# Four gate tiles between the heads of the linear attention, and another order of the expert groups

## The reference, cut to what matters

```
h = rmsnorm(x, norm1_w) * (1 + sc1) + sh1
u, gate_b, gate_c, q, k, v, g_out, lr_f, lr_b, gate_br_conv, gate_br_gla = split(h @ w_in)
y_conv = gate_b * conv3_rows(gate_c * u)
y_gla  = gla_mixer(q, k, v, g_out, ...)          # 4 heads, 2 directions, chunks of 64
merged = sigmoid(gate_br_conv) * (y_conv @ w_br_conv) + sigmoid(gate_br_gla) * (y_gla @ w_br_gla)
x = x + g1 * (merged @ w_out)
h2 = rmsnorm(x, norm2_w) * (1 + sc2) + sh2
x = x + g2 * (sum over 8 of 64 experts: w * (silu(h2 @ w_gate_e) * (h2 @ w_up_e)) @ w_down_e  + shared expert)
y = rmsnorm(x, final_norm_w)
```

## Time and profile before

| | us |
|---|---|
| median of three runs | 1001.86 |
| lowest, highest | 999.89, 1004.59 |
| profiled execution, device time | 1002.71 |
| its span, first to last instruction | 1001.0 |
| PE busy in the span | 915.7 |
| DVE busy | 436.7 |
| heads, from L1863 to the last L1898 | 188.9 to 223.05 |
| expert groups on PE | 436.7 to 965.4 |
| last pieces landed | 986.6 |

### The profile page before, as it was taken

How to read it: one execution, slowest core, us unless ns; L and a number is a source line. 1 busy time by engine, 2 the same in 40 slices (tenths; PEclk the granted TensorE clock), 3 DMA queues, 4 the chain that set the end, 5 groups by cost and what they waited for, 6 DMA issues and landing times.

```text
span 1001.0 us, 12889 instructions
## 1 busy us (share of the span) xinstructions
PE 915.7 (91%) x4821; PEld 477.9 (48%) x4821; DVE 436.7 (44%) x753; ACT 186.6 (19%) x283; POOL 104.3 (10%) x210
## 2 busy tenths in 40 slices
PE   4999999989999999999999999988979897989786
PEld 0455567675555588544444444433434343434232
DVE  3229866569542343624344333332332232332256
ACT  2140501111000002212122221211211121221111
POOL 2000000000000000201222211220221111221100
PEclk9999999999999999999999999998999998999898
DMA  9932463408558397989999999999999999999994
GB/s 374 285 121 84 147 231 130 165 1 263 200 193 312 98 381 321 397 356 406 364 372 422 421 419 419 420 420 421 419 420 422 420 419 421 420 421 421 422 418 195
DMA packets 82384, 324.24 MB, mean 324 GB/s; under 512 B 10350, under 2 KB 39194, under 8 KB 52368
## 3 DMA queue, kind: packets, MB, share of 16 engines
q1 hardware_dynamic: 66864, 289.43, 72.6%
q0 software_dynamic: 10080, 24.44, 6.3%
q10 hardware_dynamic: 5376, 9.52, 2.7%
HBM read 301.52 MB, written 34.11 MB: 335 GB/s over the span
## 4 chain that ended last, share of the span: by engine, by line
PE 82%; DMA 5%; issue 5%; DVE 4%; ACT 2%; SPq 1%; DVEq 0%
PE bank L556 26%; PE bank L1759 21%; PE bank L585 13%; PE bank L1931 4%; PE bank L1918 4%; DMA arena<-expert_rows 3%; DMA arena<-in_w_mod_dram 2%; PE bank L543 2%; PE bank L1958 2%; PE bank L1833 2%; ACT arena L567 1%; PE bank L574 1%; DVE arena L570 1%; PE bank L516 1%; PE bank L2019 1%
## 5 line engine op out<-in xcount | busy, mean ns | idle before, releaser
L556 PE MATMUL bank<-arena 128*32 128x512 f32 (+2 forms) x1536 | 268.9, 617 | 33.1 <-issue 32.0
L1759 PE MATMUL bank<-arena 128*128 128x384 f32 x640 | 208.0, 487 | 0.0
L556 PEld LDWEIGHTS bank<-arena 128*32 128x32 f32 (+2 forms) x1536 | 94.6, 128 | 204.0 <-issue 204.0
L1759 PEld LDWEIGHTS bank<-arena 128*128 128x128 f32 x640 | 121.3, 190 | 86.1 <-issue 2.6
L585 PE MATMUL bank<-arena 128*32 128x512 f32 (+2 forms) x768 | 133.2, 600 | 6.6 <-issue 5.9
L585 PEld LDWEIGHTS bank<-arena 128*32 128x32 f32 (+2 forms) x768 | 45.2, 124 | 71.4 <-issue 71.4
L430 DVE SCALAR_TENSOR_TENSOR arena<-arena 128x2048 f32<-128x2048 f32 x28 | 64.6, 2348 | 28.6 <-DMA arena<-in_w_mod_dram 27.6
L590 DVE SCALAR_TENSOR_TENSOR arena<-bank,arena 128x512 f32<-128x512 f32 x36 | 27.0, 751 | 109.7 <-PE bank L585 109.6
L598 ACT ACTIVATE arena<-arena 128x1024 f32<-128x1024 f32 x36 | 41.3, 1148 | 166.3 <-DVE arena L594 163.7
L570 DVE TENSOR_TENSOR arena<-arena,bank 128x256 f32<-128x256 f32 x36 | 21.8, 605 | 113.6 <-ACT arena L567 113.6
L530 POOL DMA_INDIRECT arena<-h_rows,arena x36 | 38.2, 1061 | 239.8 <-issue 125.1
(11 more groups left out here) (256 smaller groups left out, 732.3 us busy)
## 6 DMA issues: line engine op xcount, KB each, us to landing
arena<-in_w_gate_e_dram SPq DMA_DIRECT2D x64, 1024.0 KB
arena<-in_w_up_e_dram SPq DMA_DIRECT2D x64, 1024.0 KB
arena<-in_w_down_e_dram SPq DMA_DIRECT2D x64, 1024.0 KB
arena<-in_w_mod_dram SPq DMA_DIRECT2D x24, 1024.0 KB, 7.3
arena<-in_w_in_dram SPq DMA_DIRECT2D x22, 1024.0 KB, 6.0
expert_rows<-arena SPq DMA_DIRECT2D x6, 2048.0 KB, 23.5
arena<-expert_rows SPq DMA_DIRECT2D x12, 1024.0 KB, 25.8
arena<-in_w_out_dram SPq DMA_DIRECT2D x4, 1024.0 KB, 5.3
```

The costliest lines, as they stand in the source:

```text
L556: ins = pe.matmul(bank[off:off + width, :], x_T[:, k, off:off + width], w[:, :, k, :], start=(k == 0), stop=(k == KT - 1))
L1759: ins = pe.matmul(ps[:, 0:TOK], w[:, k, P * (n % 2):P * (n % 2) + P], hT[:, k, :], start=(k == 0), stop=(k == KT - 1))
```

## The change

Three edits.

1. **Gate tiles in the heads.** Tiles 0 to 3 of `gbc` move from behind the heads into them, one per head, in two halves of four matmuls (`project_part`): one half ahead of L1885, one ahead of the first L1898. ACT takes the sigmoid of each tile ahead of its square of the head. In `plan_jobs` the job `("gbc", h)` stands ahead of `("o", h)`, so nine jobs of a head go round eight banks. `plan_units` is not touched.
2. **Order of groups.** Experts 0 and 1 now have 96 rows each and share a group with rank 63 and rank 62 in 32 rows. Ranks 2 to 9 are the singles (eight instead of six), and there are still 36 groups. Groups 0 and 1 are the fixed pairs, 2 to 5 are pairs, singles stand at groups 6, 9, 13, 17, 21, 24, 28 and 32. SP loads ranks 63 and 62 first, each with gate, up and down.
3. **Overflow count.** Three more small DVE instructions take off 32 rows for the fixed ranks.

```diff
-BIG, MIDDLE = FIXED + 6, FIXED + 22
+BIG, MIDDLE = FIXED + 8, FIXED + 22
...
-    fixed = [[(r, 0, 128)] for r in range(FIXED)]
+    def wide_and_narrow(i, r, q):
+        return [(r, 32, 96), (q, 0, 32)] if i % 2 else [(r, 0, 96), (q, 96, 32)]
+
+    fixed = [wide_and_narrow(i, i, NE - 1 - i) for i in range(FIXED)]
...
-    first = [pairs.pop(0), fixed[0], pairs.pop(0), fixed[1], pairs.pop(0)]
+    first = fixed + [pairs.pop(0) for i in range(4)]
...
-NARROW = NE - (MIDDLE - BIG)
+NARROW = NE - FIXED - (MIDDLE - BIG)
...
-        jobs += [("o", h)]
+        jobs += [("gbc", h), ("o", h)]
...
-    jobs += [("gbc", n) for n in range(KT)]
+    jobs += [("gbc", n) for n in range(NH, KT)]
...
             for r, e in zip(first, ids):
                 load_gate_up(sp, x, e, slot_of[r])
-            for r, e in zip(first, ids):
                 load_down(sp, x, e, slot_of[r])
...
-            for edge in (MIDDLE, BIG):
-                ins = dve.tensor_scalar(above, bank(job)[:, 0:NE], float(edge), 32.0, ALU.is_lt, ALU.mult)
-                if edge == BIG:
+            for edge, rows in ((MIDDLE, 32.0), (BIG, 32.0), (FIXED, -32.0)):
+                ins = dve.tensor_scalar(above, bank(job)[:, 0:NE], float(edge), rows, ALU.is_lt, ALU.mult)
+                if edge == FIXED:
...
             for h in range(NH):
-
+                gate("gbc", g_conv, [h])
                 full(act, ("o", h))
...
-            gate("gbc", g_conv)
+            gate("gbc", g_conv, range(NH, KT))
...
+            def project_part(name, n, first, last):
+                job, u = (name, n), (name, n // 2)
+                ps = bank(job) if first else start(job)
+                arrived(u)
+                w = unit_view(u)
+                for k in range(first, last):
+                    ins = pe.matmul(ps[:, 0:TOK], w[:, k, P * (n % 2):P * (n % 2) + P], hT[:, k, :],
+                                    start=(k == 0), stop=(k == KT - 1))
+                if last == KT:
+                    finish(ins, job)
...
+                project_part("gbc", h, 0, 4)
                 job = ("o", h)
                 ps = start(job)
...
+                project_part("gbc", h, 4, KT)
                 for d in range(2):
                     if d and h + 1 < NH:
                         chunk_scores(h + 1)
...
-            project("gbc", KT)
+            project("gbc", KT, NH)
```

More of the change, by code:

```diff
@@ L61 @@
 PRIOR = 65536.0
-BIG, MIDDLE = FIXED + 6, FIXED + 22
+BIG, MIDDLE = FIXED + 8, FIXED + 22
 def plan_quads():
-    fixed = [[(r, 0, 128)] for r in range(FIXED)]
+    def wide_and_narrow(i, r, q):
+        return [(r, 32, 96), (q, 0, 32)] if i % 2 else [(r, 0, 96), (q, 96, 32)]
+    fixed = [wide_and_narrow(i, i, NE - 1 - i) for i in range(FIXED)]
     big = [[(r, 0, 128)] for r in range(FIXED, BIG)]
[L69 to L74, removed]
+    pairs = [wide_and_narrow(i, BIG + i, NE - 1 - FIXED - i) for i in range(MIDDLE - BIG)]
+    narrow = NE - 1 - FIXED - len(pairs)
+    for i in range((narrow + 1 - MIDDLE) // 2):
         r, q = MIDDLE + i, narrow - i
         pairs.append([(r, 64, 64), (q, 0, 64)] if i % 2 else [(r, 0, 64), (q, 64, 64)])
-    first = [pairs.pop(0), fixed[0], pairs.pop(0), fixed[1], pairs.pop(0)]
+    first = fixed + [pairs.pop(0) for i in range(4)]
     n, m = len(big) + len(pairs), len(big)
@@ L607, in sp_experts @@
             sp.wait_ge(S["order_ready"], 1)
-            first, second, third = [[r for r, off, width in quad] for quad in QUADS if quad[0][0] >= FIXED][:3]
+            first = [r for quad in QUADS[:FIXED] for r, off, width in quad if r >= FIXED]
+            second, third = [[r for r, off, width in quad] for quad in QUADS[FIXED:FIXED + 2]]
             def number(r):
@@ L1607, in _, with gate @@
                     free(act.activation(k_tail[:, d, h, :], bank(("kt", d, h))[:, 0:TOK], ACT.Copy), ("kt", d, h))
+            def gate(name, dst, tiles=range(KT)):
+                for n in tiles:
+                    full(act, (name, n))
+                    free(act.activation(dst[:, n, :], bank((name, n))[:, 0:TOK], ACT.Sigmoid), (name, n))
             for h in range(NH):
+                gate("gbc", g_conv, [h])
                 full(act, ("o", h))
@@ L1749, in sum_modulation @@
                 finish(ins, job)
+            def project_part(name, n, first, last):
[8 more added lines that the diff above has]
+                    finish(ins, job)
             def project(name, ncols, first=0):
                 for n in range(first, ncols):
[L1754 to L1761, removed]
+                    project_part(name, n, 0, KT)
             def transpose_in(k):
```

## The result

The changed kernel takes 1008.05 us (median of 20 runs), the kernel before took 1003.50 us in the same comparison (20 runs). The ratio is 1.0033, with an interval of 1.0020 to 1.0046, so 3.3 us slower, 2.0 to 4.6. The two medians as they stand are 4.55 us apart, near the upper end of the interval. In each set of 20 one execution stood far off (5258.57 us before, and 1086.12 us after with a granted clock of 0.846) and is left out of the ratio. The difference is more than nothing and less than the 0.5% that the prediction took as the least that can be told from no change. The forecast was +5.6 us. The profiled execution of after has a device time of 1007.97 us and a span of 1006.2 us, 5.2 us more than the span of before.

What follows compares the result with a forecast made beforehand. PE and its waits bound the front, the stream of expert weights the second half. Front +8.2, clock +2.3 and loop -4.9 make +5.6 us: 1008.3 us, or 1007.5 us held to the median, range 1003 to 1011.5.

Steps and rivals of the forecast that it cites:

- Heads: Four attention heads: four gate tiles cost 20.6 us, plus 0.4 for starts, minus 4.3 of covered waits, ending 16.7 us later.
- The term of the waits: In the heads, PE's waits ahead of L1898 (2.4 us) and L1885 (1.9 us) are all covered: 4.3 us.
- rival (b): The heads turn sour: banks or ACT's order add 1 to 2 us per head, 6 in all, 1013 us; chance 10%.
- The late unit: Behind the heads: unit of gate tiles 6 and 7 issued 18.5 us after they end, so PE waits 12.1 us.
- Rival (a): The unit of tiles 6 and 7 is not late, PE only gains, 993 us; chance 7%.
- The clock: Tiles behind PE's 12 us wait in the front start at the 1.2 GHz level: +2.3 us, 0 to 3.0.
- Rival (d): Front wait shorter and warm: unit lands in under 5 us, clock holds, loop gains 6.5 us, 1003 us; chance 10%.
- Behind the heads in all: From heads' end to modulation sum: 65.3 us instead of 73.8, so 8.5 us back, with the clock's +2.3 us against it.
- The pick on POOL: Start of the loop: one more pick for group 1 brings DVE's products and PE's second table 1.0 us later.
- The loop: Expert loop: pairs in groups 0 to 5 regain 5.9 us of idle DMA; with POOL's +1.0, -4.9 us.
- rival (c): The loop's gain does not come: DMA idles at later singles or the stream loses efficiency, 1013 us; chance 8%.
- the middle case: Whole kernel within about 0.5%, 5 us, of no change, neither under 996.9 nor over 1006.9 us; chance 0.37.

Runs made afterwards that it cites:

- experiment 3: Changed kernel with slices of the third modulation group later in the unit order, so the unit of gate tiles 6 and 7 takes another ring place: 992.09 us, ratio 0.9874.
- experiment 8: Changed kernel with two gate tiles in the heads instead of four: 999.71 us, ratio 0.9957 to the kernel before.
- experiment 4: Changed kernel with 18 extra matmuls of 128x384, results overwritten, in PE's wait for the late unit: 1003.12 us, ratio 0.9987 to the kernel before.
- experiment 2: Kernel before with only the four gate tiles in the heads, without the new groups: 1011.73 us, ratio 1.0074.
- experiment 1: Changed kernel with the gate tiles back behind the heads, the new order of groups kept: 998.88 us, ratio 0.9938 to the kernel before.
- experiment 5: Changed kernel with two pairs instead of four ahead of the first single, singles at groups 4, 8, 12: 1007.78 us, ratio 1.0047 to the kernel before.
- experiment 9: Kernel before with three more pairs behind expert 1's group and later singles, experts 0 and 1 still alone: 1004.74 us, ratio 1.0004.

## Where the prediction was right and wrong

**Heads, +16.7 forecast, +14.9 measured: the step that was off.** The term of the waits was 4.3 us, and it was too small. All of the listed waits went, but the row of waits isn't all that a wait costs. In the chain of the kernel before, the same ten matmuls stand once behind a wait for DVE and once without:

```profile
202.67 1.33 PE bank L1898 x10
204.00 1.39 PE bank L1863 x12
205.39 1.08 PE bank L1898 x10
```

In after both take 1.06 us. So a wait carries about 0.25 us of start with it, and eight waits some 2.0 us. With the 4.3 us that is 6.3 us. Measured are 4 x 5.36 - 14.86 = 6.6 us, where 5.36 us is a tile in the head (2.78 + 2.58). Of the 6.6 us 0.2 are no waits: in after PE came to the heads 0.2 us earlier (L1863 at 188.92, L1867 at 188.72). In the timeline the ten matmuls themselves take 1.33 us behind the wait and 1.23 without. The other 0.15 us is overlap: a block that needn't wait starts that much before the modelled end of the one ahead. The 0.4 us that I added for starts behind other shapes is 0.8 us (5.36 against 5.16 per tile). No bank, no read-out of DVE and no sigmoid held PE up: rival (b), the heads that turn sour, is refuted by the gapless chain.

**The late unit: right.** Distance 18.5 forecast and 18.50 measured, landing 5.24 us after the issue (5.5 taken), wait 12.01 us (12.1). The Trainium skill's figure for 1 MB (DMA: Bandwidth & Descriptors, section Bandwidth), 6.15 us, was further off than the rows. SP had issued nothing for 44 us ahead of this unit, and it issued the next one 0.42 us behind it. Experiments 3 and 8 show that the cause is the ring place and the little work left behind the heads: with another place the wait goes, with two more tiles behind the heads 1.39 us of it are left. That the distance hangs on DVE and ACT alone is not quite so: in experiment 8 PE's sums were slower and it was 19.03 us. Rival (a), the unit that is not late, is refuted.

**The clock: right.** 2.3 us were taken from six blocks of the loop; the block behind the wait lost 2.26 us to 8 x 5.16, and 2.0 us to experiment 4. The agreement to 0.1 us is luck: behind the same wait the loss was 3.0 us in experiment 2. Rival (d), a short and warm wait, is refuted for the wait of 12 us; experiment 8 shows it for one of 1.4 us.

**Behind the heads in all:** -8.5 + 2.3 = -6.2 forecast, 8.47 - 14.86 = -6.4 measured.

**The pick on POOL, +1.0 forecast, +0.6 measured.** The picks ahead of the first gather, after:

```profile
428.43 0.19 POOL L506 COPY arena<-arena 128x12 f32 x1 [0.88 <-issue]
...
429.35 0.19 POOL L506 COPY arena<-arena 128x12 f32 x1 [0.45 <-issue]
430.05 0.19 POOL L506 COPY arena<-arena 128x12 f32 x1 [0.50 <-issue]
430.33 0.20 POOL L674 TENSOR_SCALAR arena<-arena 128x3 f32<-128x3 f32 x1
...
432.06 1.05 PE L516 MATMUL bank<-arena 128*32 128x4 f32 x18 [1.16 <-DVE arena L524]
```

A pick costs 0.7 us here (429.35 to 430.05), not the 1.1 of the earlier trace rows. PE's second table shifts by 432.06 - 423.36 = 8.70, the first gate and up by 9.04, where the front had shifted by 8.47. So POOL's picks make only 0.2 of the 0.6 us. Another 0.25 is the larger table itself, 1.05 us instead of 0.80, which stands on the chain and which the prediction put at nothing.

**The loop: right size, half a cause.** -5.9 us forecast for the stream, -5.7 measured from first gate and up to the last piece, and experiment 1 shows it as a gain of 6.2 us by itself. But I put it down to groups 1, 3 and 5, and the forecast of rival (c) to where the singles are. Experiments 5 and 9 show that the place of the first singles does not matter: the loss goes with the fixed experts standing alone. Pairing them came together with the new order of the first loads (each new expert's down right behind its gate and up), and no run parts the two. A reason that fits, argued and not shown: experts 0 and 1 sit loaded in slots when the loop begins. At that time DMA has all slots full, and a group that frees one slot for 13 us of PE cannot feed it. A few groups later DMA is behind, and a single is a chance to catch up. Rival (c), no gain in the loop, is refuted.

**The sum.** With the measured terms: 14.9 - 6.4 + 0.6 - 5.7 = +3.4 us at the last piece, which is the ratio measured, 3.3 us. The forecast of +5.6 was 2.2 us over it, of which the heads make 1.8 and POOL 0.4. With it went the chances: slower by over 0.5% had the largest, 0.56, and did not come; what came is the middle case, which had 0.37. The sum stood just above the bound, and the heads' 1.8 us carried it over. The heads ended at 237.9 instead of "near 240", the sum of the modulation came at 305.3 instead of 307, the loop shrank by 5.7 within the 4 to 7 us, and the slices between 480 and 530 are at 407 to 424 GB/s, one of them under the 415 I asked for. What the prediction did not speak of is the tail. There PE's sums can take over the end from the transfers, 1.9 us in the profiled execution. So it is luck that the span, at +5.2 us, looks closer to the forecast than its parts: the tail's 1.9 us stand against the 1.8 us of the heads. One reading of the earlier trace rows was wrong as well and changed nothing in the sum: in the first 500 us DMA moves 1 to 406 GB/s, not 84 to 381; the slice with 1 is that of the heads. The level of 1007.5 us came close to 1008.05 us partly by chance, since the kernel before was measured at 1003.50 and not at 1001.86 in that comparison.

## What to carry to other kernels

Work moved forward in front of a fixed point of another engine also moves the use of everything behind it forward. Before filling waits with such work, look up in the ring who frees the place of each load that the moved work leaves behind: here a place freed 18.5 us after the heads turned a gain of about 8 us into a loss of 7 to 10 (experiment 2, and after against experiment 1), and one line that orders the loads turned it back. In a loop fed by a stream, look at the first groups, where the buffers are all full: here it paid to let what already sits loaded share its group with a second expert, so that each group frees two buffers.

## What was not expected of the hardware

- A short wait of PE costs more than its idle time: ten small matmuls behind a wait of 0.5 us took 1.33 us of the chain, without one 1.06 to 1.08. The ends of matmuls are modelled, so this is a difference of the chain's pieces.
- The length of a short wait does not tell whether the clock falls. A wait of 1.39 us, and one of 0.55, cost none (eight tiles in 41.52 us). But waits of 0.50 and 0.62 us at the end of the heads cost 1.5 us in experiment 8 and nothing in before, and behind the same wait of 1.28 us ahead of the output projection the next block took 13.87 us in experiment 4 and 15.55 in after. A wait of 12 us cost the clock in each of the three profiles that have one: 2.0 to 3.0 us.
- Ahead of the final sums PE stands for 0 to 3.8 us, from one kernel to the next. Behind the gaps of 3.48 to 3.78 us, for which the profile shows no releaser, the first block took 9.76 to 10.09 us in six of seven profiles and 7.11 in the seventh (experiment 1). In before and experiment 2 the gap is 2.1 us, but the last down block ahead of it is shown 1.6 to 1.7 us longer: from that block's start to the sums it is 7.1 to 7.4 us in these nine profiles. What PE is held by there stays open.
